# Feed-forward of a two-layer decoder: low parts of eight sample columns placed beside their high parts in one moving row

## What is computed

```
def swiglu(x, w_in, w_out):
    gate, up = jnp.split(x @ w_in, 2, axis=-1)
    return (jax.nn.silu(gate) * up) @ w_out
...
    h = x + 0.5 * rms_norm(swiglu(rms_norm(x, p['n_ffn1_pre']), p['ffn1_w_in'], p['ffn1_w_out']), p['n_ffn1_post'])
    m, s_ret, s_gdn, conv_buf = token_mixing(rms_norm(h, p['n_mix_pre']), pos, mem_k, mem_v, ...)
    h = h + rms_norm(m, p['n_mix_post'])
    h = h + 0.5 * rms_norm(swiglu(rms_norm(h, p['n_ffn2_pre']), p['ffn2_w_in'], p['ffn2_w_out']), p['n_ffn2_post'])
```

## Time and profile before

| | |
|---|---|
| median of 3 runs | 1825.12 us (1823.24 to 1826.16) |
| the profiled execution | 1824.02 us, of which 1822.2 us from its first instruction to its last |
| TensorE busy | 1785.0 us, 98% of the span |
| VectorE, ScalarE busy | 72%, 49% |
| granted TensorE clock, mean | 0.999 of full |

### The profile page before, as it was taken

One profiled execution on the slowest core, in us unless ns is written; L12 is line 12 of the kernel. 1 busy time (PEld: TensorE's weight loads), 2 busy tenths in 40 slices (PEclk: granted clock), 3 DMA queues, 4 the chain that ended last, 5 costly groups with the idle time before them and its releaser, 6 DMA issues.

```text
span 1822.2 us, 40358 instructions
## 1 busy us (share of the span) xinstructions
PE 1785.0 (98%) x16247; PEld 1724.7 (95%) x16247; DVE 1304.2 (72%) x2063; ACT 888.4 (49%) x1052; POOL 140.3 (8%) x214
## 2 busy tenths in 40 slices
PE   7999999999999999999999999999999999999998
PEld 6999999988889999999999999999889899999998
DVE  6677566787777877777567765778776776877764
ACT  5444354556564354543354334555566534454343
POOL 0100002211210100000000000131112010000000
PEclk9999999999999999999999999999999999999999
DMA  6876668976775656666667766697778475446654
GB/s 195 243 217 198 176 194 269 300 232 222 268 233 163 200 181 214 177 187 168 173 199 215 208 191 183 189 332 248 236 237 280 159 225 180 163 139 192 181 166 136
DMA packets 436433, 376.65 MB, mean 207 GB/s; under 512 B 10098, under 2 KB 411892, under 8 KB 435626
## 3 DMA queue, kind: packets, MB, share of 16 engines
q1 hardware_dynamic: 409560, 276.60, 50.8%
q0 software_dynamic: 26688, 97.48, 15.7%
HBM read 347.29 MB, written 26.76 MB: 205 GB/s over the span
## 4 chain that ended last, share of the span: by engine, by line
PE 78%; DVE 8%; ACT 6%; DMA 4%; issue 4%; SPq 0%; DVEq 0%; ACTq 0%
PE proj L719 52%; PE proj L737 4%; PE proj L742 4%; PE proj L738 4%; ACT wh L1404 3%; PE proj L693 2%; DVE wl L1903 2%; PE proj L717 2%; PE aux L784 2%; PE aux L931 2%; DMA raw<-ffn_w_out 1%; DMA raw<-ffn_w_in 1%; PE aux L1100 1%; PE aux L880 1%; PE aux L896 1%
## 5 line engine op out<-in xcount | busy, mean ns | idle before, releaser
L1903 DVE TENSOR_TENSOR wl<-raw,wh 128x2048 fp32r<-128x2048 f32 (+1 forms) x280 | 599.2, 2140 | 208.2 <-ACT wh L1404 184.8
L1404 ACT CAST wh<-raw 128x2048 fp32r<-128x2048 f32 (+1 forms) x280 | 500.2, 1786 | 264.7 <-PE proj L719 113.0
L719 PE MATMUL proj<-xh,wh 128*128 128x264 f32 x2624 | 383.9, 288 | 2.5 <-ACT wh L1404 2.5
L719 PE MATMUL proj<-xl,wh 128*128 128x264 f32 x2624 | 381.3, 285 | 0.0
L719 PE MATMUL proj<-xh,wl 128*128 128x264 f32 x2624 | 371.7, 284 | 4.2 <-DVE wl L1903 3.9
L719 PEld LDWEIGHTS proj<-xl,wh 128*128 128x128 f32 x2624 | 341.3, 188 | 12.9 <-issue 12.3
L719 PEld LDWEIGHTS proj<-xh,wh 128*128 128x128 f32 x2624 | 341.1, 188 | 6.0 <-ACT wh L1404 2.7
L719 PEld LDWEIGHTS proj<-xh,wl 128*128 128x128 f32 x2624 | 338.8, 188 | 5.8 <-DVE wl L1903 5.5
L737 PE MATMUL proj<-hh,wh 128*128 128x264 f32 x704 | 173.7, 284 | 0.0
L738 PE MATMUL proj<-hl,wh 128*128 128x264 f32 x704 | 173.4, 283 | 0.0
L1425 ACT ACTIVATE gate<-gate 128x264 f32<-128x264 f32 x88 | 37.4, 425 | 242.8 <-DVEq L1938 242.7
(11 more groups left out here) (477 smaller groups left out, 2186.1 us busy)
## 6 DMA issues: line engine op xcount, KB each, us to landing
raw<-ffn_w_in SPq DMA_DIRECT2D x176, 512.0 KB, 5.2
raw<-w_in SPq DMA_DIRECT2D x80, 1024.0 KB, 5.8
raw<-ffn_w_out SPq DMA_DIRECT2D x64, 704.0 KB, 4.6
sring<-cache_mem_k POOLq DMA_DIRECT2D x32, 512.0 KB, 6.2
sring<-cache_mem_v POOLq DMA_DIRECT2D x32, 512.0 KB, 5.0
out<-sring POOLq DMA_DIRECT2D x32, 512.0 KB, 4.5
sring<-state_gdn POOLq DMA_DIRECT2D x30, 512.0 KB, 5.6
raw<-w_mem_v SPq DMA_DIRECT2D x8, 1024.0 KB, 6.3
```

The costliest lines, as they stand in the source:

```text
L719: mm = pe.matmul(o, w[:, s, k * 256 + t * P:k * 256 + (t + 1) * P], a[:, k, :], **go)
L1404: act.copy(wh[:, slot, 0:size], raw[:, slot, 0:size]).then_inc(hi_done[slot], 1)
L1903: dve.tensor_sub(wl[:, slot, 0:size], raw[:, slot, 0:size], wh[:, slot, 0:size].bitcast(F32)).then_inc(split_done[slot], 1)
```

## The change

`xh`, `hh`, `gate`, `tmpf` and `rt` get rows of TB = 272 columns. The last 8 hold, beside the 264 of before, the low parts of the 8 samples (in `rt` a second copy of the samples' norm). The HIGH matmuls of the feed-forward then move 272 columns and leave two partial sums for the samples, columns 256 to 263 and 264 to 271; the INPUT_LOW matmuls move the prompt's 256 alone; the WEIGHT_LOW matmuls move 264 as before. VectorE adds the two partial sums: in `hidden_tile` after either scaling, in `result_tile` by a reduction over the pairs, with the samples' squares made there and ScalarE's square cut to 256 columns. The first group of each `f1i` and `f2i` is left as it was. `hl` rows have 256 columns. The zone begins 448 bytes later on each partition, 32 of them a tile `zone_start` that nothing reads.

```diff
+TB = T + NS
...
-        xh, xl = sb("xh", [P, KT, T], F32R), sb("xl", [P, KT, T], F32R)
+        xhb, xl = sb("xh", [P, KT, TB], F32R), sb("xl", [P, KT, T], F32R)
+        xh = xhb[:, :, 0:T]
...
+        sb("zone_start", [P, 8])
         ZONE = 91776
...
-        hh = at("hh", 0, [P, FT, T], F32R)
-        hl = at("hl", FT * T * 4, [P, FT, T], F32R)
+        hh = at("hh", 0, [P, FT, TB], F32R)
+        hl = at("hl", FT * TB * 4, [P, FT, SEQ], F32R)
...
+                                if beside is not None:
+                                    a = beside if part == HIGH else a[:, :, 0:SEQ] if part == INPUT_LOW else a
...
-                                        mm = pe.matmul(o, w[:, s, k * 256 + t * P:k * 256 + (t + 1) * P], a[:, k, :], **go)
+                                        mm = pe.matmul(o[:, 0:a.shape[2]], w[:, s, k * 256 + t * P:k * 256 + (t + 1) * P], a[:, k, :], **go)
...
                             pe.matmul(o, w, high[:, kk, :], start=(kk == 0), stop=False)
-                            pe.matmul(o, w, low[:, kk, :], start=False, stop=False)
+                            pe.matmul(o[:, 0:SEQ], w, low[:, kk, :], start=False, stop=False)
...
-                            mm = pe.matmul(o, wl[:, s, k * P:(k + 1) * P], high[:, kk, :], start=False, stop=(kk == FT - 1))
+                            mm = pe.matmul(o[:, 0:T], wl[:, s, k * P:(k + 1) * P], high[:, kk, 0:T], start=False, stop=(kk == FT - 1))
...
-                        order(act.activation(sqt[:, slot, :], proj[bank][:, 0:T], ACT.Square))
+                        columns = T if ph.tiles else SEQ
+                        order(act.activation(sqt[:, slot, 0:columns], proj[bank][:, 0:columns], ACT.Square))
...
                     if j == 0:
                         norm_wait(dve, l, "rt", n)
+                        order(cp(rtb[:, T:TB], rt[:, SEQ:T]))
+                    columns = TB if j else T
+
+                    def scaled(t, out):
+                        bank = tile_wait(dve, l, ph, i, u, t)
+                        order(tt(out[:, 0:columns], proj[bank][:, 0:columns], rtb[:, 0:columns], ALU.mult))
+                        dve.sem_inc(bank_free[bank], 1)
+                        if j:
+                            order(tt(out[:, SEQ:T], out[:, SEQ:T], out[:, T:TB], ALU.add))
+                    scaled(0, gateb[:, u % 2, :])
                     dve.sem_inc(product_scaled, 1)
+                    scaled(1, tmpb)
...
-                    parts(hh[:, j, :], hl[:, j, :], tmpf[:])
+                    order(cp(hh[:, j, 0:T], tmpf[:]))
+                    order.apart(tt(hl[:, j, :], tmpf[:, 0:SEQ], hh[:, j, 0:SEQ].bitcast(F32), ALU.subtract))
+                    order.apart(tt(hh[:, j, T:TB], tmpf[:, SEQ:T], hh[:, j, SEQ:T].bitcast(F32), ALU.subtract))
+                    order.wait()
...
+                        if not ph.tiles:
+                            order(dve.tensor_reduce(own[:], proj[bank][:, SEQ:TB].rearrange("p (a b) -> p b a", a=2), AX.X, ALU.add))
+                            order(tt(sqt[:, slot, SEQ:T], own[:], own[:], ALU.mult))
+                            if j == KT - 1:
+                                dve.sem_inc(M[done], 1)
+                            order(ts_(y[:, j, SEQ:T], own[:], gl[:, j, gain:gain + 1], None, ALU.mult))
+                        order(ts_(y[:, j, 0:columns], proj[bank][:, 0:columns], gl[:, j, gain:gain + 1], None, ALU.mult))
...
                     order.wait()
+                    if half and n != 2:
+                        order(cp(xhb[:, :, T:TB], xl[:, :, SEQ:T].bitcast(F32)))
                     dve.sem_inc(M[f"xn{n}"], 1)
```

More of the change, by code:

```diff
@@ L164, in build @@
         erow = sb("erow", [P, H, P])
-        gate = sb("gate", [P, 2, T])
+        gateb = sb("gate", [P, 2, TB])
+        gate = gateb[:, :, 0:T]
         sqt = sb("sqt", [P, 2, T])
-        tmpf = sb("tmpf", [P, T])
-        acc, rt = sb("acc", [P, T]), sb("rt", [P, T])
+        tmpb = sb("tmpf", [P, TB])
+        tmpf = tmpb[:, 0:T]
+        acc, rtb = sb("acc", [P, T]), sb("rt", [P, TB])
+        rt = rtb[:, 0:T]
+        own = sb("own", [P, NS])
         full = sb("full", [P, 2, SEQ + 3])
@@ L670, in end, with products @@
                 mm.then_inc(aux_full[PLACE[name][0]], 1)
-            def products(l, name, high, low, kind="", after=None, branch=None, groups=None, mid=None, inner=None, early=None, parts_of=None):
+            def products(l, name, high, low, kind="", after=None, branch=None, groups=None, mid=None, inner=None, early=None, parts_of=None, beside=None):
                 def group(ph, i, u):
@@ L704, in group @@
                             hi_, lo_ = (low if isinstance(low, tuple) and u % 2 else high) if kind == "mix" else (high, low)
-                            o = proj[bank][:, 0:256 if kind == "natural" else hi_.shape[2]]
+                            o = proj[bank][:, 0:256 if kind == "natural" else TB if beside is not None else hi_.shape[2]]
                             done = 0
@@ L728, in group @@
                         bank = u // 2
-                        o = proj[bank][:, 0:T]
+                        o = proj[bank][:, 0:TB]
                         if u % 2 == 0:
@@ L835, in _ @@
                 products(l, "mvb", memh, meml, "natural", mid=last_result)
-                products(l, "f1i", xh, xl, early=halves(1), parts_of=unscaled(1))
+                products(l, "f1i", xh, xl, early=halves(1), parts_of=unscaled(1), beside=xhb)
                 products(l, "f1o", hh, hl, early=hidden_tiles(0))
@@ L1321, in _ @@
                     keep_streaming(l, "n3", 14)
-                products(l, "f2i", xh, xl, early=halves(3), parts_of=unscaled(3))
+                products(l, "f2i", xh, xl, early=halves(3), parts_of=unscaled(3), beside=xhb)
                 products(l, "f2o", hh, hl, early=hidden_tiles(1))
@@ L1934, in tile @@
                         norm_wait(dve, l, "rt", n)
-                    bank = tile_wait(dve, l, ph, i, u, 0)
-                    order(tt(gate[:, u % 2, :], proj[bank][:, 0:T], rt[:], ALU.mult))
-                    dve.sem_inc(bank_free[bank], 1)
+                        order(cp(rtb[:, T:TB], rt[:, SEQ:T]))
[7 more added lines that the diff above has]
+                    scaled(0, gateb[:, u % 2, :])
                     dve.sem_inc(product_scaled, 1)
-                    bank = tile_wait(dve, l, ph, i, u, 1)
-                    order(tt(tmpf[:], proj[bank][:, 0:T], rt[:], ALU.mult))
-                    dve.sem_inc(bank_free[bank], 1)
+                    scaled(1, tmpb)
                     dve.wait_ge(gate_ready, l * ACT_TILES + GATE0[ph.name] + j + 1)
@@ L1956, in tile @@
                         bank = tile_wait(dve, l, ph, i, u, t)
+                        columns = T if ph.tiles else SEQ
                         dve.wait_ge(sq_ready, l * 24 + SQ0[ph.name] + j + 1)
-                        order(ts_(y[:, j, :], proj[bank][:, 0:T], gl[:, j, gain:gain + 1], None, ALU.mult))
+                        if not ph.tiles:
[5 more added lines that the diff above has]
+                        order(ts_(y[:, j, 0:columns], proj[bank][:, 0:columns], gl[:, j, gain:gain + 1], None, ALU.mult))
                         if j < KT - 1:
                             order(tt(acc[:], acc[:], sqt[:, slot, :], ALU.add))
-                            if j == KT - 2:
+                            if ph.tiles and j == KT - 2:
                                 dve.sem_inc(M[done], 1)
```

## The result

The changed kernel takes 1833.69 us (median of 4 runs, 1833.10 to 1835.62), the kernel before, beside it on the same chip, 1824.18 (1822.73 to 1826.16). The ratio is 1.0050, 95% interval 1.0038 to 1.0062: slower by half a per cent. The forecast was 1818.7, with a range up to 1829. Of the rivals, the ninth line (1835.4) came nearest. The profiled execution of the changed kernel took 1835.62 us, span 1833.8. Two single executions in the experiments were far slower (1931.38 and 7609.74 us), and medians are given without them.

A forecast was written before the change was run, and what follows sets the result against it. TensorE's matmul spacing was taken as the bound: 1824.0 us, less 7.5 for half the start rule, plus 1.1 of costs, gave 1817.6; with the median 1.1 above the profiled execution, 1818.7 us, range 1809 to 1829.

The forecast's parts named there:

- the ninth line: Rival, 11%: 272 columns pay another 7.4 ns step and cost 128.1 ns, 9.2 us more, 1835.4 us; decides from about 125 ns.
- the rule on starts at multiples of 128 bytes: Moving rows starting at multiples of 128 bytes cost 6.6 ns over their columns, others 11.1; full 17.3 us saved, half taken.
- the sum's term of -7.5 us: TensorE's gain from half the start rule, 8.6 us, less half of the mixer's share, 1.1.
- `f1i`, `f2i`: Feed-forward products in: three matmuls 357.8 ns against 362.1, 4.3 less for 1344 triples, 5.8 us by the full rule.
- `f1o`, `f2o`: Feed-forward products out: 9.8 ns less for 704 triples, 6.9 us by the full rule, 5.2 after the third phase's transfers.
- mixer: Mixer's projections, 2560 matmuls on `xh`: 1.8 ns less each, 4.6 us by the full rule.
- `mk`: 384 matmuls over both layers in `mk`: 4.5 ns less each, 1.7 us by the full rule.
- if a matmul cost its columns and a constant: Constant-overhead rival, 26%: column count stays 792, so TensorE gains nothing and only the costs remain, 1826.2 us.
- The loop: VectorE and ScalarE turn in `f1i`, `f2i`: from 5.38 to 5.65 us, still covered by TensorE's 5.76.
- The end: Behind the last square, the sum on TensorE waits for a reduction and a 128x8 product: 0.4 us more.
- The first feed-forward: Three longer turns before the load that takes 11.0 us: 0 to 0.8 us later, taken as 0.4.
- The third feed-forward: Copy of `rt`'s 8 columns goes before the split for group 2: 0.2 us later.

The follow-up runs named there:

- (1): No layer, 50 streams of 64 matmuls alone, each with one width and one pair of start residues: 113.4 ns each for 256 columns at 192 bytes.
- (7): Matmul streams alone, high and low rows side by side in 2304-byte rows: 22.98 to 23.62 us; best placement then put into three whole kernels, 1824.20 to 1829.81 us.
- (4): Four feed-forward groups alone at the kernels' own addresses: layout before 23.20 us, changed 23.39, changed with 264 columns throughout 23.36, before with low rows cut to 256 23.20.
- (2): Zone begins 64 bytes later: changed kernel 1832.46 us (1.0041 to the kernel before), kernel before 1827.33 us (1.0014).
- (5): Changed kernel without VectorE's two additions of the samples' second partial products in each hidden tile: 1832.63 us, ratio to the kernel before 1.0048.
- the placed kernel: Change with high and low rows side by side in 2304-byte rows, low at 192, high at 0: 1827.47 us for products into the hidden layer alone, 1829.81 whole.
- the placed whole change: Whole change with high and low rows side by side in 2304-byte rows, low at 192, high at 0: 1829.81 us, ratio to the kernel before 1.0021.
- the placed in-only kernel: Change in the products into the hidden layer alone, rows side by side, low at 192, high at 0: 1827.47 us, ratio to the kernel before 1.0013.
- the placed kernel before: Kernel before, matmuls unchanged, rows side by side in 2304-byte rows, low at 192, high at 224: 1824.20 us, ratio to the kernel before 0.9992.
- out only: Change in the two products out of the hidden layer alone, zone start modulo 256 bytes as in the kernel before: 1825.04 us, ratio 1.0003.
- (8): Placed whole change without VectorE's two additions: 1827.34 us, ratio 1.0013; also second profiles of both kernels unchanged, first `f1i` 133.64 us before and 134.87 changed.

## Why the prediction was wrong

**The failed step is the rule on starts at multiples of 128 bytes**, and with it the sum's term of -7.5 us. It was read from one pair of rows and already fitted two others badly; taking half of it kept its sign. In place of it the runs showed spacings that change with the moving row's start against the stationary tile, with nothing special at 128 (1), in a way that no run turned into a price list (7), and a new layout that makes 0.16 of the 0.19 us lost in four groups (4). Term by term:
- `f1i`, `f2i`: forecast 2.2 ns less for three matmuls (half of 4.3); measured 365.8 against 362.5, 3.3 more: 1.1 to 1.2 us a phase, about 4.6 us in four.
- `f1o`, `f2o`: forecast -2.6 us; measured +0.2 in each phase, 0.75 in all.
- mixer: forecast -1.2; measured +0.8 in `gq` and `gz` alone, and some tenths in phases with stops.
- `mk`: forecast -0.9; measured +0.28 in the first layer. In the second the first profile of the kernel before has a stop that its second has not; against that one it is +0.28 again.
- natural phases: not priced; measured +1.6, shown to be the zone's start (2).

That is about +8 in place of -7.5. In the sum for `f1o` a quarter was struck off because the third phase seemed to take 66.3 us, set by its transfers. That was a misreading of the earlier trace rows: the stretch of 66.3 us runs 2.4 us into `mk`. From the phase's first matmul to the first of `mk`, with the columns of the earlier trace rows, it is

```profile
1069.68:1133.83 64.15, 64.15 (x531) 64.05 (x529) 32.58 (x35) 26.51 (x24) 0.00 (x0) 1.00 0.64 188
```

and the first phase takes 64.10, so transfers cost TensorE nothing there. One sentence of the prediction was right as a condition: if a matmul cost its columns and a constant, TensorE would gain nothing; and the ninth line's threshold of about 125 ns for 272 columns was met (125 to 126), with 256 at 119, not 117.8. But that rival's reason, a step from one width to the next, is only half of it: at residue 192 the same 272 columns cost 123.3 (1). That its 1835.4 lies near the measured time is in part luck: it had 6.0 us from `f1i` and `f2i`, 3.2 from `f1o` and `f2o`, and nothing for the natural phases.

**The loop** was right: 5.62 us a turn against 5.65, and TensorE stays slower. What was missed is how the smaller slack shows: the loop starts late in each phase and catches up 0.23 us a turn (5.85 - 5.62) instead of 0.41, so one stop stays in the fifth group, 0.1 to 0.2 us in each of the last three phases (5).

**The other costs.** The end: 0.4 forecast, 0.36 read from the rows. The first feed-forward: 0.4 forecast; with the clock's fall and the spacing taken off, 0.1 to 0.4 remain. The third feed-forward: 0.2 forecast for the split of its third group. That group took 5.99 and 5.91 us in the two profiles before and 5.88 in both after, like the fourth: nothing was lost there. Its first group took 8.09 and 7.73 us, 7.77 and 7.83 before, which is chance.

**Not foreseen: a fall of the clock.** In the second layer's `x0` (`x01`) the changed kernel loses 1.14 us. Timeline of the last matmuls of a chain of small ones, and windows behind them, first the changed kernel, then its second profile, then the kernel before:

```profile
1445.45 0.25 PE L1109 MATMUL aux<-blk_t,blk_y 32*32 32x32 f32 x4 [1.70 <-issue]
```

```profile
1446.60:1449.40 2.80, 2.80 (x14) 2.34 (x13) 1.65 (x2) 1.72 (x2) 0.00 (x0) 0.50 0.10 30
```

```profile
1443.87 0.25 PE L1109 MATMUL aux<-blk_t,blk_y 32*32 32x32 f32 x4 [1.42 <-issue]
```

```profile
1445.10:1447.90 2.80, 2.80 (x31) 2.23 (x33) 1.84 (x2) 2.07 (x2) 0.00 (x0) 0.50 0.07 16
```

```profile
1436.85 0.25 PE L1100 MATMUL aux<-blk_t,blk_y 32*32 32x32 f32 x4 [1.50 <-issue]
```

```profile
1437.40:1440.20 2.80, 2.80 (x84) 2.52 (x82) 2.36 (x2) 1.53 (x2) 0.00 (x0) 1.00 0.07 26
```

Behind an idle time of 1.70 us, and in the second profile of only 1.42, the granted clock was 0.50; behind one of 1.50 in the kernel before it stayed at 1.00. So the length of the idle time does not decide it. Five of six profiles with the whole change have this fall there, none of the eight others. The same phase of the first layer has such a fall in four profiles, three of them without the change, so the 1.1 us may be chance. What brings the fall stays open.

The sum: 8 for spacing, 0.5 for the loop's stops, 0.4 for the end, 1.1 in `x01`, and 1.1 of chance in the first `f1i` make 11.1, against 11.6 between the two profiles and 9.5 between the medians.

**What stays open.** Why the placed kernel leaves its fast spacing behind the fifth group, with the same operands at the same addresses. A stop is not needed for such a step: without the additions (5) the last `f2i` of the changed kernel goes from 5.88 us a group to 5.85 on average at the fifth, which stops for nothing (5.869, as the ninth). Nor is it the moment at which VectorE splits: in the placed whole change's second feed-forward the split begins 4.0 us into the sixth group and 3.0 into the thirteenth, and the groups go on at 5.82, 5.81, 5.81 and 5.78 in turn. So something counts beside the residue, and no run takes that apart. By an estimate from these groups it costs some 4 us (0.06 us, 17 groups, four phases), without which the placed in-only kernel would stand below the kernel before. As it is, no version with the change beat the kernel before; the placed kernel before is 0.08% faster by its median ratio with an interval that ends at 1.0001, so it can't be called faster.

## What to carry to other kernels

Count neither columns nor a constant for a matmul whose rows change length: let the new shapes run alone at the addresses that they will have, since a change of layout alone can cost more than the columns give (here 0.16 us in four groups, where 8 columns less in 64 matmuls gave 0.00). An edit that makes one buffer longer moves every buffer behind it; price the phases that read those, or keep their starts modulo 256 bytes (with the zone 64 bytes later the natural phases of the kernel before took 1.41 us more, with the zone 256 bytes later, out only, 0.07). And where a term rests on a rule read from one pair of rows which other rows contradict, its sign is as open as its size.

## What the runs showed of the hardware

- Matmuls of float32r with 256, 264 and 272 columns at a granted clock of 1.00 start 6.7 to 16.7 ns over their columns apart, by the start of the moving row modulo 256 bytes against that of the stationary tile, and by width (1): 113.3 to 120.0 ns for 256 columns, 120.0 to 126.7 for 264, 123.3 to 126.7 for 272. One width at one clock has several values.
- At a granted clock of 0.50 they start 220.0 ns apart with 264 columns and 212.5 with 256 (8), 0.83 ns a column and nothing on top.
- Eight columns more or less can change nothing: 192 matmuls took 23.20 us with 64 of them at 264 or at 256 columns (4).
- The same eight matmuls, at the same addresses, took 0.918 us in the first groups of a phase and 0.941 from the sixth on (7); what makes the difference is open.
- Stops of TensorE of 1.4 to 2.5 us were followed, in some executions, by a stretch at a granted clock of 0.50 (2.2 and 2.8 us of it in the windows above); stops as long were not, in others. One such fall costs about 1.1 us, so a single profile can differ by that much from the next of the same kernel.
